# The end of a decoder step on one core: scaling of the output shared between VectorE and GpSimd, and a shorter path to the norm's factor

## The chip, the core and the metric

The kernel is written in Bass and runs on one core of one Trainium2 chip. The core has a matrix engine (TensorE, PE in the profile, PEld where it loads weights), a vector engine (VectorE, DVE), a scalar engine (ScalarE, ACT), a general engine (GpSimd, POOL) and a sequencer that only issues transfers (SyncE, SP). Engines wait for each other through semaphores. The metric is the device time of one execution in microseconds (us).

## The reference, cut to what matters

One layer of a hybrid decoder is computed for 256 prompt rows and 8 x 8 sample rows, together 320 tokens of width 2048: a norm, one wide input projection, three attention branches, three gated branch projections, an output projection with the residual added, and a final norm. The change is in the last step alone:

```
y = x + merged @ w_out                                     # (320, 2048)
inv = rsqrt(mean(y * y, axis=-1) + 1e-6)                    # one factor for each token
y_prompt, y_sample = y * inv * final_norm_g
```

## The kernel before, in words

Everything is transposed: the width lies on the 128 partitions in 16 blocks (KB), and the tokens lie along the free dimension. Weights come as a stream of tiles of 128 x 2048; ScalarE and VectorE split each tile into a high and a low part (lines 494 and 753), and TensorE multiplies high by high, high by low and low by high (lines 1263 to 1265). The output projection makes two of the 16 blocks per trip; VectorE adds each to the residual in y_t (line 1162), GpSimd squares it and adds the squares up in y_ss (lines 479 and 481), and ScalarE multiplies it by the gain of the final norm into y_out (line 718, semaphore y_gained).

The last two blocks are handled by hand, and in two halves of 160 tokens (h = 0 and h = 1), so that the final scaling of the first half can begin while TensorE still works on the second. In y_out a "half block" is thus 128 partitions x 160 tokens, there are 32 of them, and each is 81.92 KB in float32. For each half:

- VectorE adds the products to y_t (half_added, lines 1178 and 1179), adds the square of block 14 to the sums (rest_summed, line 1188) and squares block 15 (last_square, line 1193). ScalarE squares block 14 (line 728) and applies the gains (line 724).
- TensorE sums over the partitions by products with ones into two columns of the bank S0 (lines 1620, 1629, 1632; semaphore y_ssd): the tokens are then on the partitions, 128 in a column.
- VectorE makes mean + eps from them (mean, line 1199), ScalarE takes the square root (line 743), VectorE takes the reciprocal and makes one Newton step (newton, lines 1203 to 1206) and writes the result on the diagonal of a 128 x 128 matrix (y_diag, line 1210).
- TensorE multiplies ones by that diagonal (factor_products, line 1608; semaphore y_inv), which puts the factor of each token on all partitions of a bank: S1 for h = 0, P0 for h = 1.
- VectorE multiplies y_out by it in place, in ten parts (scaled, line 1217, the list OUT_PARTS of half, first and last block), reading the factor from PSUM, and SP stores each part when it is done (line 397).

The order on VectorE is written out by hand: newton(0), half_added(0, 1), scaled(0), rest_summed(1), half_added(1, 1), last_square(1), scaled(1), mean(1), scaled(2), newton(1), and then parts 3 to 9. Parts 0 to 4 are the first half of the tokens, 5 to 9 the second. GpSimd has nothing to do after its last sum of squares.

Of the kernel before, what the change touches and what calls it, by code (L numbers as in the profile page):

```python
# [12 lines left out]
P = 128  # L13
D_MODEL, SEQ, DEC_BATCH, DEC_SEQ, PAST, PAGE = 2048, 256, 8, 8, 256, 128
# [4 lines left out]
EPS = 1e-6  # L19
NEG = -1e30  # L20
KB = D_MODEL // P
# [13 lines left out]
NGP = 32  # L35
FIRST_SEQS = 5
HALF = TOK // 2
OUT_PARTS = ((0, 0, 2), (0, 2, 6), (0, 6, 8), (0, 8, 12), (0, 12, 16), (1, 0, 4), (1, 4, 8), (1, 8, 12), (1, 12, 14), (1, 14, 16))
HEAD = ((0, 2), (2, 4), (4, 8), (8, 12), (12, 16))

f32 = mybir.dt.float32
# [2 lines left out]
ALU = mybir.AluOpType  # L44
ACT = mybir.ActivationFunctionType
# [33 lines left out]
def build(nc, A):  # L79
    ctx = ExitStack()  # L80
    with ctx:
# [24 lines left out]
        ident = fixed("ident", [P, P])  # L106
        ones = fixed("ones", [P, P])
# [11 lines left out]
        st = fixed("st", [P, 16])  # L119
# [96 lines left out]
        y_last = fixed("y_last", [P, 4, HALF])  # L216
        y_sum = fixed("y_sum", [P, 2, HALF])
        y_diag = fixed("y_diag", [P, 2, P])

        bank = [ctx.enter_context(nc.psum_tensor(f"bank{n}", [P, 512], f32)) for n in range(8)]  # L220
        W, (S0, S1, S2, P0, P1, OB) = bank[:2], bank[2:]
# [5 lines left out]
        def two(name):  # L227
# [22 lines left out]
         brow_copied, bo_ready, bo_copied, pad_zero, new_zero, pc_zero, pb_zero, bias_in) = [  # L250
            sem(n) for n in ("b_staged kt_in vs_in bs_ready bvc_rdy bmax_rdy bexp_done bp_ready bpt_ready bpt_copied "
                             "brow_ready brow_copied bo_ready bo_copied pad_zero new_zero pc_zero pb_zero bias_in").split()]
        (oz_rdy, oz_hi_rdy, oz_lo_rdy, mrg_rdy, mrg_hi_rdy, mrg_lo_rdy, y_in, y_sums, y_half, y_put, y_pres, y_squared, y_ssd, y_v, y_r, y_turned, y_inv, y_gained, y_rdy, y_wr) = [
            sem(n) for n in ("oz_rdy oz_hi_rdy oz_lo_rdy mrg_rdy mrg_hi_rdy mrg_lo_rdy y_in y_sums y_half y_put y_pres y_squared y_ssd y_v y_r "
                             "y_turned y_inv y_gained y_rdy y_wr").split()]
        dve_chain = sem("dve_chain")
        carrier = sem("carrier")

# [32 lines left out]
        def _(sp):  # L291
# [100 lines left out]
                    load_keys(b + 2)  # L392
            weight_tile(1, J_MRG + 1)
            weight_tiles(J_MRG + 2, J_END)
            for n, (h, k0, k1) in enumerate(OUT_PARTS):
                sp.wait_ge(y_rdy, n + 1)
                sp.dma_start(A["y_out"][h, :, k0:k1, :], y_out[:, h, k0:k1, :]).then_inc(y_wr, 16)
            sp.wait_ge(y_wr, 16 * len(OUT_PARTS))


        @block.gpsimd
        def _(pool):
# [73 lines left out]
            with pool.Fori(0, KB // 2 - 1) as k:  # L476
                for u in range(2):
                    pool.wait_ge(w_free[u], k + (J_OUT + 2))
                    nc.gpsimd.tensor_tensor(y_sq[:, u, :], one(y_t, k * 2 + u), one(y_t, k * 2 + u), ALU.mult).then_inc(y_sums, 1)
                    pool.wait_ge(y_sums, k * 4 + (2 * u + 2))  # L480
                    nc.gpsimd.tensor_tensor(y_ss[:], y_ss[:], y_sq[:, u, :], ALU.add).then_inc(y_sums, 1)
            pool.wait_ge(win_wr, 16 * DEC_BATCH)
            pool.wait_ge(kv_out, 32)
            for u in range(2):
# [4 lines left out]
        def _(act):  # L489
# [226 lines left out]
            def gained_block(kb):  # L716
                act.wait_ge(w_free[kb % 2], kb // 2 + (J_OUT + 2))
                nc.scalar.activation(y_out[:, :, kb, :], y_t[:, kb, :].rearrange("p (h c) -> p h c", h=2), ACT.Copy,
                                     scale=gains[:, 2, kb:kb + 1]).then_inc(y_gained, 1)

            def gained_half(u, h):
                kb = KB - 2 + u
                act.wait_ge(y_put, 2 * h + u + 1)
                nc.scalar.activation(y_out[:, h, kb, :], y_t[:, kb, h * HALF:(h + 1) * HALF], ACT.Copy, scale=gains[:, 2, kb:kb + 1]).then_inc(y_gained, 1)

            def squared_half(h):
                act.wait_ge(y_put, 2 * h + 1)
                nc.scalar.activation(y_last[:, 2 * h, :], y_t[:, KB - 2, h * HALF:(h + 1) * HALF], ACT.Square).then_inc(y_squared, 1)
# [6 lines left out]
                        gained_block(2 * k - 2 + u)  # L735
            for kb in range(KB - 4, KB - 2):
                gained_block(kb)
            for h in range(2):
                squared_half(h)
                gained_half(0, h)  # L740
                gained_half(1, h)
                act.wait_ge(y_v, h + 1)
                nc.scalar.activation(st[:, 3:5], st[:, 0:2], ACT.Sqrt).then_inc(y_r, 1)


        @block.vector
        def _(dve):
# [447 lines left out]
            v, y, t = st[:, 0:2], st[:, 3:5], st[:, 6:8]  # L1195

            def mean(h):
                dve.wait_ge(y_ssd, h + 1)
                nc.vector.tensor_scalar(v, S0[:, 256 * h:256 * h + 2], 1.0 / D_MODEL, EPS, ALU.mult, ALU.add).then_inc(y_v, 1)

            def newton(h):
                dve.wait_ge(y_r, h + 1)
                ch.link(nc.vector.reciprocal(y, y))
                ch.link(nc.vector.scalar_tensor_tensor(t, y, -0.5, y, ALU.mult, ALU.mult))
                ch.link(nc.vector.tensor_tensor(t, t, v, ALU.mult))
                ch.link(nc.vector.scalar_tensor_tensor(y, t, 1.5, y, ALU.add, ALU.mult))
                if h:
                    dve.wait_ge(y_inv, 1)
                for n in range(2):
                    nc.vector.tensor_scalar_mul(y_diag[:, n, :], ident[:], st[:, 3 + n:4 + n]).then_inc(y_turned, 1)  # L1210

            def scaled(n):
                h, k0, k1 = OUT_PARTS[n]
                out = y_out[:, h, k0:k1, :]
                dve.wait_ge(y_gained, KB if h == 0 else KB + 2)
                dve.wait_ge(y_inv, h + 1)
                nc.vector.tensor_tensor(out, out, (S1, P0)[h][:, 0:HALF].unsqueeze(1).to_broadcast([P, k1 - k0, HALF]),
                                        ALU.mult).then_inc(y_rdy, 1)

            dve.wait_ge(y_half, 1)  # L1220
            ch.link(half_added(0, 0))
            dve.wait_ge(y_half, 2)
# [8 lines left out]
            mean(0)  # L1231
            newton(0)
            dve.wait_ge(y_half, 5)
            half_added(0, 1).then_inc(y_put, 1)
# [3 lines left out]
            half_added(1, 1).then_inc(y_put, 1)  # L1238
            last_square(1).then_inc(y_pres, 1)
            scaled(1)  # L1240
            mean(1)
            scaled(2)
            newton(1)
            scaled(3)
            scaled(4)
            for n in range(5, len(OUT_PARTS)):
                scaled(n)


# [1 line left out]
        def _(pe):  # L1251
# [350 lines left out]

            firsts = (0, HALF - P)

            def factor_products(h):
                for n, (c0, c1) in enumerate(((0, P), (P, HALF))):
                    pe.wait_ge(y_turned, 2 * h + n + 1)
                    mm = nc.tensor.matmul((S1, P0)[h][:, c0:c1], ones[:], y_diag[:, n, P - (c1 - c0):P], start=True, stop=True)
                mm.then_inc(y_inv, 1)

            for u in range(2):
# [12 lines left out]
            factor_products(0)  # L1624
            half_part(1, 1, range(9, KB))
            pe.wait_ge(y_v, 1)
            pe.wait_ge(y_pres, 2)
# [3 lines left out]
            for n, first in enumerate(firsts):  # L1631
                mm = nc.tensor.matmul(S0[:, 256 + n:257 + n], y_last[:, 3, first:first + P], ones[:, 0:1], start=False, stop=True, skip_group_check=True)
            mm.then_inc(y_ssd, 1)
            factor_products(1)


# [107 lines left out]
```

## Time and profile before

| what | value |
|---|---|
| median of 3 runs | 1124.12 us (1123.13 to 1125.02) |
| the profiled execution's own time | 1123.93 us |
| its span, first to last instruction | 1122.1 us |
| time outside the span | 1.83 us |
| PE busy | 1110.0 us (99%) |
| DVE busy | 620.2 us (55%) |
| ACT busy | 422.4 us (38%) |
| POOL busy | 63.6 us (6%) |
| granted TensorE clock, mean | 0.996 |

The time is that of a whole execution; the rows of the trace count from the start of the span. Busy time says how long an engine had work, not whether that work set the end. In the rows, names are those of the program (bank stands for any PSUM bank), and "[0.69 <-DVE y_last L1193]" is the idle time before an instruction and what ended it. A float32 product of TensorE shows as two records.

### The profile page before, as it was taken

How to read it: one execution, taken by the hardware profiler on the slowest of the kernel's cores; microseconds unless marked ns; L12 is line 12 of the kernel's file. 1: busy time of each engine (PE TensorE's matmuls, PEld its weight loads, DVE VectorE, ACT ScalarE, POOL GpSimd, SP SyncE). 2: the span in 40 equal slices, each digit the busy share in tenths (PEclk: the TensorE clock that was granted, in tenths of full speed). 3: DMA queues.
4: the chain of work that ended last, by engine and by line, in shares of the span. 5: the costliest groups of instructions: out<-in, count | busy, mean ns of one | idle time of the engine just before them, and what ended most of it. 6: DMA issues, size and time to landing. Idle time of an engine off the chain costs nothing.

```text
span 1122.1 us, 19565 instructions
## 1 busy us (share of the span) xinstructions
PE 1110.0 (99%) x8092; PEld 1086.1 (97%) x8092; DVE 620.2 (55%) x914; ACT 422.4 (38%) x573; POOL 63.6 (6%) x111
## 2 busy tenths in 40 slices
PE   9999999999999999999999999999999999999996
PEld 7998999999999999999999999999999999999996
DVE  5974443536446767675555567454454454454445
ACT  6633322424335445443333334333333333333332
POOL 0014000000000000000000000000000000002220
PEclk9999999999999999999999999999999999999998
DMA  8545775544545233349787834544444444464442
GB/s 289 191 168 193 245 262 192 188 149 151 172 137 185 79 114 109 114 162 311 246 299 262 271 121 167 171 168 168 170 168 169 169 150 149 151 243 148 150 150 94
DMA packets 63467, 201.79 MB, mean 180 GB/s; under 512 B 6448, under 2 KB 35184, under 8 KB 45088
## 3 DMA queue, kind: packets, MB, share of 16 engines
q1 hardware_dynamic: 58688, 186.50, 48.4%
q0 software_dynamic: 2400, 10.89, 2.8%
q10 hardware_dynamic: 2304, 3.34, 0.9%
q8 instruction: 55, 0.90, 0.3%
q14 instruction: 20, 0.16, 0.0%
HBM read 193.48 MB, written 11.41 MB: 183 GB/s over the span
## 4 chain that ended last, share of the span: by engine, by line
PE 92%; DVE 4%; DMA 2%; ACT 1%; issue 1%; SPq 1%; DVEq 0%; ACTq 0%
PE bank L1263 26%; PE bank L1265 26%; PE bank L1264 26%; DMA raw<-in_stream 2%; DVE w_lo L753 1%; PE bank L1594 1%; PE bank L1368 1%; PE bank L1363 1%; PE bank L1340 1%; PE bank L1342 1%; PE bank L1341 1%; PE bank L1490 1%; DVE m_lo L780 1%; ACT w_hi L494 1%; PE bank L1425 0%
## 5 line engine op out<-in xcount | busy, mean ns | idle before, releaser
L494 ACT ACTIVATE w_hi<-raw 128x2048 fp32r<-128x2048 f32 x141 | 270.0, 1915 | 580.5 <-PE bank L1265 535.6
L1263 PE MATMUL bank<-h_hi,w_hi 128*128 128x320 f32 x1552 | 484.9, 312 | 0.5 <-DVE w_lo L753 0.5
L1265 PE MATMUL bank<-h_hi,w_lo 128*128 128x320 f32 x1552 | 479.6, 309 | 0.0
L1264 PE MATMUL bank<-h_lo,w_hi 128*128 128x320 f32 x1552 | 479.5, 309 | 0.0
L753 DVE TENSOR_TENSOR w_lo<-raw,w_hi 128x2048 fp32r<-128x2048 f32 x141 | 327.6, 2323 | 178.5 <-ACT w_hi L494 178.4
L1263 PEld LDWEIGHTS bank<-h_hi,w_hi 128*128 128x128 f32 x1552 | 291.5, 188 | 5.4 <-issue 3.9
L1264 PEld LDWEIGHTS bank<-h_lo,w_hi 128*128 128x128 f32 x1552 | 291.5, 188 | 0.4
L1265 PEld LDWEIGHTS bank<-h_hi,w_lo 128*128 128x128 f32 x1552 | 291.3, 188 | 0.0
L1264 PE MATMUL bank<-oz_lo,w_hi 128*128 128x320 f32 x256 | 78.9, 308 | 0.0
L1265 PE MATMUL bank<-oz_hi,w_lo 128*128 128x320 f32 x256 | 78.8, 308 | 0.0
L1263 PE MATMUL bank<-oz_hi,w_hi 128*128 128x320 f32 x256 | 78.8, 308 | 0.0
L1263 PE MATMUL bank<-mrg_both,w_hi 128*128 128x320 f32 x224 | 69.0, 308 | 0.0
L1264 PE MATMUL bank<-mrg_both,w_hi 128*128 128x320 f32 x224 | 69.0, 308 | 0.0
L1265 PE MATMUL bank<-mrg_both,w_lo 128*128 128x320 f32 x224 | 69.0, 308 | 0.0
L1137 DVE TENSOR_TENSOR g<-bank,inv 128x320 f32<-128x320 f32 x32 | 15.7, 490 | 72.2 <-PE bank L1265 72.2
L1263 PEld LDWEIGHTS bank<-oz_hi,w_hi 128*128 128x128 f32 x256 | 48.0, 188 | 0.0
L1264 PEld LDWEIGHTS bank<-oz_lo,w_hi 128*128 128x128 f32 x256 | 48.0, 188 | 0.0
L1265 PEld LDWEIGHTS bank<-oz_hi,w_lo 128*128 128x128 f32 x256 | 48.0, 188 | 0.0
L1263 PEld LDWEIGHTS bank<-mrg_both,w_hi 128*128 128x128 f32 x224 | 42.0, 188 | 0.0
L1264 PEld LDWEIGHTS bank<-mrg_both,w_hi 128*128 128x128 f32 x224 | 42.0, 188 | 0.0
L1265 PEld LDWEIGHTS bank<-mrg_both,w_lo 128*128 128x128 f32 x224 | 42.0, 188 | 0.0
L1094 DVE TENSOR_TENSOR g_t<-bank,inv 128x320 f32<-128x320 f32 x16 | 7.9, 492 | 42.4 <-PE bank L1265 42.4
(341 smaller groups left out, 1137.7 us busy)
## 6 DMA issues: line engine op xcount, KB each, us to landing
raw<-in_stream SPq DMA_DIRECT2D x141, 1024.0 KB, 5.0
cmp_t<-in_cmp_pages SPq DMA_DIRECT2D x32, 128.0 KB, 4.2
kt_moba<-in_moba_k SPq DMA_DIRECT2D x16, 256.0 KB, 5.3
kt_mem<-in_mem_k SPq DMA_DIRECT2D x8, 512.0 KB, 6.2
vs_moba<-in_moba_v SPq DMA_DIRECT2D x16, 256.0 KB
vs_mem<-in_mem_v SPq DMA_DIRECT2D x8, 512.0 KB
out_win_old<-in_cache_win POOLq DMA_DIRECT2D x8, 512.0 KB, 3.6
raw<-in_stream SPq DMA_DIRECT2D x11, 256.0 KB, 9.1
```

Source lines behind the costliest of these rows:

```text
L494: nc.scalar.activation(w_hi[:, u], raw[:, u], ACT.Copy).then_inc(hi_ready[u], 1)
L753: nc.vector.tensor_tensor(w_lo[:, u], raw[:, u], w_hi[:, u].bitcast(f32), ALU.subtract).then_inc(lo_ready[u], 1)
L780: nc.vector.scalar_tensor_tensor(lo[:, kb, :], x[:, kb, :], gains[:, gain, kb:kb + 1], hi[:, kb, :].bitcast(f32), ALU.mult, ALU.subtract). ...
L1137: nc.vector.tensor_tensor(g12[:, u, br, :], W[u][:, 0:TOK], inv[:], ALU.mult).then_inc(w_free[u], 1)
L1263: nc.tensor.matmul(out[:, 0:n], w_hi[:, u, kb, :], hi[:, kb, :], start=(kb == first), stop=False)
L1264: nc.tensor.matmul(out[:, 0:n], w_hi[:, u, kb, :], lo[:, kb, :], start=False, stop=False)
L1265: mm = nc.tensor.matmul(out[:, 0:n], w_lo[:, u, kb, :], hi[:, kb, :], start=False, stop=(kb == last))
L1340: nc.tensor.matmul(out[:], m_hi[:, kb, rows], high, start=(kb == 0), stop=False)
L1341: nc.tensor.matmul(out[:], m_lo[:, kb, rows], high, start=False, stop=False)
L1342: mm = nc.tensor.matmul(out[:], m_hi[:, kb, rows], low, start=False, stop=(kb == KB - 1))
L1363: nc.tensor.matmul(out[:, 0:used], w_hi[:, 1, s, :], c_hi[:, s, 0:used], start=(s == 0), stop=False, skip_group_check=True)
L1368: mm = nc.tensor.matmul(out[:, 0:used], w_lo[:, 1, s, :], c_hi[:, s, 0:used], start=False, stop=(s == CMP_STRIDE - 1), skip_group_check=True)
```

## The change

OUT_PARTS is split in two lists. VectorE keeps 18 half blocks in six parts, GpSimd gets 14 in three. The factor of each half is also copied by ScalarE from PSUM to a tile y_fac in SBUF, which GpSimd reads, and VectorE too for the first half; for the second half VectorE reads P0 as before, and TensorE makes the factor a second time in P1 for the copy. The square root is taken on ScalarE straight from the sums in PSUM, with 1 / D_MODEL as its scale and eps as its bias. The last operation of the Newton step is done by the instruction that writes the diagonal. TensorE makes five products of ones between the last sums and the factor. SP stores eight of the nine parts in the order DVE 0, DVE 1, POOL 0, POOL 1, DVE 2 to 5; ScalarE's queue stores POOL 2.

```diff
-OUT_PARTS = ((0, 0, 2), (0, 2, 6), (0, 6, 8), (0, 8, 12), (0, 12, 16), (1, 0, 4), (1, 4, 8), (1, 8, 12), (1, 12, 14), (1, 14, 16))
+OUT_DVE = ((0, 0, 2), (0, 2, 6), (1, 4, 8), (1, 8, 12), (1, 12, 14), (1, 14, 16))
+OUT_POOL = ((0, 6, 11), (0, 11, 16), (1, 0, 4))
...
+        y_fac = fixed("y_fac", [P, 2, HALF])
...
@@ sync
-            for n, (h, k0, k1) in enumerate(OUT_PARTS):
-                sp.wait_ge(y_rdy, n + 1)
+            def store(ready, parts, n):
+                h, k0, k1 = parts[n]
+                sp.wait_ge(ready, n + 1)
                 sp.dma_start(A["y_out"][h, :, k0:k1, :], y_out[:, h, k0:k1, :]).then_inc(y_wr, 16)
+            for n in range(2):
+                store(y_rdy, OUT_DVE, n)
+            for n in range(2):
+                store(y_rdy_pool, OUT_POOL, n)
+            for n in range(2, len(OUT_DVE)):
+                store(y_rdy, OUT_DVE, n)
...
@@ gpsimd, after the last sum of squares
+            def scaled(n):
+                h, k0, k1 = OUT_POOL[n]
+                out = y_out[:, h, k0:k1, :]
+                pool.wait_ge(y_gained, KB if h == 0 else KB + 2)
+                pool.wait_ge(y_fac_rdy, h + 1)
+                nc.gpsimd.tensor_tensor(out, out, y_fac[:, h, :].unsqueeze(1).to_broadcast([P, k1 - k0, HALF]), ALU.mult).then_inc(y_rdy_pool, 1)
+
+            for n in range(len(OUT_POOL)):
+                scaled(n)
...
@@ scalar
+            def factor_out(h):
+                act.wait_ge(y_inv, 2 * h + 1)
+                nc.scalar.activation(y_fac[:, h, :], (S1, P1)[h][:, 0:HALF], ACT.Copy).then_inc(y_fac_rdy, 1)
+
             for h in range(2):
                 squared_half(h)
+                if h:
+                    factor_out(0)
                 gained_half(0, h)
                 gained_half(1, h)
-                act.wait_ge(y_v, h + 1)
-                nc.scalar.activation(st[:, 3:5], st[:, 0:2], ACT.Sqrt).then_inc(y_r, 1)
+                act.wait_ge(y_ssd, h + 1)
+                nc.scalar.activation(st[:, 3:5], S0[:, 256 * h:256 * h + 2], ACT.Sqrt, scale=1.0 / D_MODEL, bias=st[:, 13:14]).then_inc(y_r, 1)
+            factor_out(1)
+            act.wait_ge(y_rdy_pool, 3)
+            h, k0, k1 = OUT_POOL[2]
+            act.dma_start(A["y_out"][h, :, k0:k1, :], y_out[:, h, k0:k1, :]).then_inc(y_wr, 16)
...
@@ vector
             def mean(h):
-                dve.wait_ge(y_ssd, h + 1)
                 nc.vector.tensor_scalar(v, S0[:, 256 * h:256 * h + 2], 1.0 / D_MODEL, EPS, ALU.mult, ALU.add).then_inc(y_v, 1)
...
                 ch.link(nc.vector.reciprocal(y, y))
+                mean(h)
                 ch.link(nc.vector.scalar_tensor_tensor(t, y, -0.5, y, ALU.mult, ALU.mult))
-                ch.link(nc.vector.tensor_tensor(t, t, v, ALU.mult))
-                ch.link(nc.vector.scalar_tensor_tensor(y, t, 1.5, y, ALU.add, ALU.mult))
+                nc.vector.tensor_scalar(t[:, 0:1], t[:, 0:1], v[:, 0:1], 1.5, ALU.mult, ALU.add)
+                ch.link(nc.vector.tensor_scalar(t[:, 1:2], t[:, 1:2], v[:, 1:2], 1.5, ALU.mult, ALU.add))
...
-                    nc.vector.tensor_scalar_mul(y_diag[:, n, :], ident[:], st[:, 3 + n:4 + n]).then_inc(y_turned, 1)
+                    nc.vector.tensor_scalar(y_diag[:, n, :], ident[:], y[:, n:n + 1], t[:, n:n + 1], ALU.mult, ALU.mult).then_inc(y_turned, 1)
...
-                h, k0, k1 = OUT_PARTS[n]
+                h, k0, k1 = OUT_DVE[n]
...
-                dve.wait_ge(y_inv, h + 1)
-                nc.vector.tensor_tensor(out, out, (S1, P0)[h][:, 0:HALF].unsqueeze(1).to_broadcast([P, k1 - k0, HALF]),
+                dve.wait_ge((y_fac_rdy, y_inv)[h], h + 1)
+                nc.vector.tensor_tensor(out, out, (y_fac[:, 0, :], P0[:, 0:HALF])[h].unsqueeze(1).to_broadcast([P, k1 - k0, HALF]),
                                         ALU.mult).then_inc(y_rdy, 1)
...
             last_square(1).then_inc(y_pres, 1)
             scaled(1)
-            mean(1)
-            scaled(2)
             newton(1)
-            scaled(3)
-            scaled(4)
-            for n in range(5, len(OUT_PARTS)):
+            for n in range(2, len(OUT_DVE)):
                 scaled(n)
...
@@ tensor, after the last sums
-            factor_products(1)
+            for n in range(5):
+                nc.tensor.matmul(W[0][:, 0:P], ones[:], ones[:], start=True, stop=True)
+            factor_products(1, P0)
+            factor_products(1, P1)
```

## Rows read from the trace of the kernel before

**Rows 1.** Chain of waits, its last piece: start us, us, what.

```profile
1117.48 1.53 DVE y_out L1217 x3
```

**Rows 2.** Table of stretches: busy us of each engine, PEclk, DMA share, GB/s.

```profile
1112.00:1113.50 1.50, 0.61 (x4) 0.52 (x4) 1.47 (x6) 0.42 (x2) 0.00 (x0) 1.00 0.00 0
1113.50:1115.10 1.60, 0.68 (x4) 0.69 (x4) 1.50 (x6) 0.00 (x0) 0.00 (x0) 0.50 0.80 307
1115.10:1116.10 1.00, 0.38 (x3) 0.24 (x2) 1.00 (x3) 0.00 (x0) 0.00 (x0) 0.50 0.00 0
1116.10:1121.30 5.20, 0.00 (x0) 0.00 (x0) 2.90 (x5) 0.00 (x0) 0.00 (x0) 0.50 0.97 377
```

**Rows 3.** Stores of the output: an issue on the timeline, all ten, time to landing.

```profile
1115.31 0.33 SPq L397 DMA_DIRECT2D out_y_out<-y_out  x1
...
L397 SPq DMA_DIRECT2D out_y_out<-y_out x10: 332/332/739, 1110.5 to 1119.1; - x10
...
DMA to landing us min/median/max: 1.8/2.3/2.7
```

**Rows 4.** Timeline of DVE from 1110 us: start us, us, line, operation.

```profile
1110.03 0.49 DVE L1217 TENSOR_TENSOR y_out<-y_out,bank 128x320 f32<-128x320 f32 x1 [0.45 <-PE bank L1608]
1110.43 0.32 DVE L1188 TENSOR_TENSOR y_sum<-y_ss,y_last 128x160 f32<-128x160 f32 x1
1111.07 0.33 DVE L1178 SCALAR_TENSOR_TENSOR y_t<-bank,y_t 128x160 f32<-128x160 f32 x1 [0.32 <-PE bank L1594]
...
1111.79 0.32 DVE L1193 TENSOR_TENSOR y_last<-y_t 128x160 f32<-128x160 f32 x1
1112.03 0.81 DVE L1217 TENSOR_TENSOR y_out<-y_out,bank 128x640 f32<-128x640 f32 x1
1112.81 0.16 DVE L1199 TENSOR_SCALAR st<-bank 128x2 f32<-128x2 f32 x1
...
1113.29 0.16 DVE L1203 RECIPROCAL st<-st 128x2 f32<-128x2 f32 x1
...
1114.08 0.48 DVE L1210 TENSOR_SCALAR y_diag<-ident,st 128x128 f32<-128x128 f32 x2
1114.47 4.53 DVE L1217 TENSOR_TENSOR y_out<-y_out,bank 128x640 f32<-128x640 f32 x7
```

**Rows 5.** Timeline of PE at the end, and of its first products of ones.

```profile
1109.39 0.53 PE L1608 MATMUL bank<-y_diag,ones 128*128 128x128 f32 x4
...
1112.16 0.61 PE L1632 MATMUL bank<-ones,y_last 128*128 128x1 f32 x4 [0.69 <-DVE y_last L1193]
1114.42 1.06 PE L1608 MATMUL bank<-y_diag,ones 128*128 128x128 f32 x4 [1.65 <-DVE y_diag L1210]
...
1.72 6.62 PE L1281 MATMUL bank<-ones 128*128 128x128 f32 x32 [1.72 <-DVE ones L761]
```

**Rows 6.** Timeline of ACT: a square of 160 tokens and the square root.

```profile
1109.61 0.34 ACT L728 ACTIVATE y_last<-y_t 128x160 f32<-128x160 f32 x1 [1.93 <-DVE y_t L1179]
...
1113.00 0.21 ACT L743 ACTIVATE st<-st 128x2 f32<-128x2 f32 x1 [0.79 <-DVE st L1199]
```

**Rows 7.** Groups of POOL instructions, shapes apart: busy us, mean ns of one.

```profile
L481 POOL TENSOR_TENSOR y_ss<-y_ss,y_sq 128x320 f32<-128x320 f32 x14 | 12.3, 880 | 1.1
...
L460 POOL COPY kt_moba<-k_smp 128x32 f32<-128x32 f32 x8 | 1.7, 208 | 0.0
```

**Rows 8.** Timelines of POOL and DVE: a w_lo that starts beside POOL, and one alone.

```profile
1083.44 0.88 POOL L481 TENSOR_TENSOR y_ss<-y_ss,y_sq 128x320 f32<-128x320 f32 x1
...
1083.84 2.63 DVE L753 TENSOR_TENSOR w_lo<-raw,w_hi 128x2048 fp32r<-128x2048 f32 x1 [1.40 <-ACT w_hi L494]
...
900.82 2.29 DVE L753 TENSOR_TENSOR w_lo<-raw,w_hi 128x2048 fp32r<-128x2048 f32 x1 [1.51 <-ACT w_hi L494]
```

**Rows 9.** Timelines of DVE and POOL: a POOL copy that starts beside w_lo.

```profile
518.22 2.28 DVE L753 TENSOR_TENSOR w_lo<-raw,w_hi 128x2048 fp32r<-128x2048 f32 x1
...
519.58 0.99 POOL L459 COPY kt_nsa<-k_smp 128x32 f32<-128x32 f32 x1 [18.31 <-PE bank L1483]
```

More of the change, by code:

```diff
@@ L252, in build @@
                              "brow_ready brow_copied bo_ready bo_copied pad_zero new_zero pc_zero pb_zero bias_in").split()]
-        (oz_rdy, oz_hi_rdy, oz_lo_rdy, mrg_rdy, mrg_hi_rdy, mrg_lo_rdy, y_in, y_sums, y_half, y_put, y_pres, y_squared, y_ssd, y_v, y_r, y_turned, y_inv, y_gained, y_rdy, y_wr) = [
+        (oz_rdy, oz_hi_rdy, oz_lo_rdy, mrg_rdy, mrg_hi_rdy, mrg_lo_rdy, y_in, y_sums, y_half, y_put, y_pres, y_squared, y_ssd, y_v, y_r, y_turned, y_inv, y_fac_rdy, y_gained, y_rdy, y_rdy_pool, y_wr) = [
             sem(n) for n in ("oz_rdy oz_hi_rdy oz_lo_rdy mrg_rdy mrg_hi_rdy mrg_lo_rdy y_in y_sums y_half y_put y_pres y_squared y_ssd y_v y_r "
-                             "y_turned y_inv y_gained y_rdy y_wr").split()]
+                             "y_turned y_inv y_fac_rdy y_gained y_rdy y_rdy_pool y_wr").split()]
         dve_chain = sem("dve_chain")
@@ L394, in _ @@
             weight_tiles(J_MRG + 2, J_END)
-            for n, (h, k0, k1) in enumerate(OUT_PARTS):
-                sp.wait_ge(y_rdy, n + 1)
+            def store(ready, parts, n):
+                h, k0, k1 = parts[n]
+                sp.wait_ge(ready, n + 1)
                 sp.dma_start(A["y_out"][h, :, k0:k1, :], y_out[:, h, k0:k1, :]).then_inc(y_wr, 16)
-            sp.wait_ge(y_wr, 16 * len(OUT_PARTS))
+            for n in range(2):
[4 more added lines that the diff above has]
+                store(y_rdy, OUT_DVE, n)
+            sp.wait_ge(y_wr, 16 * (len(OUT_DVE) + len(OUT_POOL)))
         @block.gpsimd
@@ L1209, in newton @@
                 for n in range(2):
-                    nc.vector.tensor_scalar_mul(y_diag[:, n, :], ident[:], st[:, 3 + n:4 + n]).then_inc(y_turned, 1)
+                    nc.vector.tensor_scalar(y_diag[:, n, :], ident[:], y[:, n:n + 1], t[:, n:n + 1], ALU.mult, ALU.mult).then_inc(y_turned, 1)
             def scaled(n):
-                h, k0, k1 = OUT_PARTS[n]
+                h, k0, k1 = OUT_DVE[n]
                 out = y_out[:, h, k0:k1, :]
                 dve.wait_ge(y_gained, KB if h == 0 else KB + 2)
-                dve.wait_ge(y_inv, h + 1)
-                nc.vector.tensor_tensor(out, out, (S1, P0)[h][:, 0:HALF].unsqueeze(1).to_broadcast([P, k1 - k0, HALF]),
+                dve.wait_ge((y_fac_rdy, y_inv)[h], h + 1)
+                nc.vector.tensor_tensor(out, out, (y_fac[:, 0, :], P0[:, 0:HALF])[h].unsqueeze(1).to_broadcast([P, k1 - k0, HALF]),
                                         ALU.mult).then_inc(y_rdy, 1)
+            nc.vector.memset(st[:, 13:14], EPS)
             dve.wait_ge(y_half, 1)
@@ L1230, in _ @@
             nc.vector.tensor_tensor(y_sum[:, 0, :], y_sum[:, 0, :], y_last[:, 1, :], ALU.add).then_inc(y_pres, 1)
-            mean(0)
             newton(0)
@@ L1603, in _, with factor_products @@
             firsts = (0, HALF - P)
-            def factor_products(h):
+            def factor_products(h, out):
                 for n, (c0, c1) in enumerate(((0, P), (P, HALF))):
                     pe.wait_ge(y_turned, 2 * h + n + 1)
-                    mm = nc.tensor.matmul((S1, P0)[h][:, c0:c1], ones[:], y_diag[:, n, P - (c1 - c0):P], start=True, stop=True)
+                    mm = nc.tensor.matmul(out[:, c0:c1], ones[:], y_diag[:, n, P - (c1 - c0):P], start=True, stop=True)
                 mm.then_inc(y_inv, 1)
@@ L1623, in _ @@
             half_part(1, 1, range(0, 9))
-            factor_products(0)
+            factor_products(0, S1)
             half_part(1, 1, range(9, KB))
```

## The prediction

> **What bounds the kernel now.** TensorE is busy for 99% of the span, but the change touches only what comes after its last large product, so I read the end alone. The chain of waits ends in VectorE's scaling [rows 1]. That names an engine, not yet the limit, so the table of stretches comes next [rows 2]: from 1116.1 to 1121.3 us the DMA engines are 97% busy at 377 GB/s. Ten stores are issued, the last at 1119.1, and each lands 1.8 to 2.7 us after its issue [rows 3]. VectorE scales the last 24 half blocks in 4.53 us [rows 4], 0.19 us each; the transfer takes 5.2 us for the same 24 (24 x 81.92 KB = 1.97 MB), 0.217 us each. So from 1116.1 on the store is the slower of the two, and the span ends 0.8 us after it has drained. The issue that restarts it is at 1115.31, the data follow 0.8 us later.
>
> The reader is to see that the DMA engines stand still from 1112.0 to 1113.5 and from 1115.1 to 1116.1 [rows 2]. A change gains only by filling these holes with ready half blocks. For any new order
>
> end of span = issue that restarts the stream + 0.8 + 0.217 x half blocks left + holes + 0.8.
>
> Check on before: 1115.3 + 0.8 + 5.2 + 0.8 = 1122.1.
>
> **The edits, one by one.**
>
> *Root straight from the sums.* The mean starts at 1112.81 [rows 4], the root at 1113.00 [rows 6]: 0.19 us leave the path. The mean then runs behind the reciprocal, inside the 0.2 us that a linked step takes.
>
> *End of the refinement in the diagonal.* From reciprocal to diagonal 0.79 us now, four linked steps of 0.2 [rows 4]. Then three linked steps and two short unlinked instructions, which I price by their spacing at 0.07 each: 0.74. Bounds: 0.6 (the two free) and 0.9 (a full 0.16 each). Gain 0.05.
>
> *PE kept warm.* The same factor products take 0.53 us in the first half and 1.06 in the second [rows 5]; the granted clock is 1.00 until 1113.5 and 0.50 behind it [rows 2], that is 2.4 and then 1.2 GHz, after TensorE had little to do since 1111 and nothing between 1112.77 and 1114.42. If the clock holds, 0.5 us is gained. The five products are ten records; 32 such records took 6.62 us at the start [rows 5], so ten take up to 2.1 us. They are hidden only while the diagonal comes later than that behind the sums.
>
> *The second factor product and the copy.* Behind the first, 0.5 to 1.1 us on TensorE (warm, cold); only GpSimd's third part waits for it. The copy is 160 wide: 0.34 us by the square of that width [rows 6]; from below 0.21, the root of two elements. For the first half it is on the path: scaled(0) now starts at 1110.03 [rows 4], right behind the product, and would start at 1110.4. The stores must start there, and rest_summed(1) is queued behind it on VectorE.
>
> *GpSimd's parts.* Its add of 320 elements takes 0.88 us, a copy of 32 elements 0.21 [rows 7]: 2.1 ns an element. A part of 800: 0.88 + 480 x 2.1 ns = 1.9 us; from above 2.2, all of it in proportion. The part of 640: 1.55 us. Two parts need 3.8 us. They can begin at 1110.5 and no engine waits for GpSimd there; the cover looks ample. VectorE keeps 12 half blocks behind the second factor, 2.3 us instead of 4.5.
>
> **The port.** Here the profile speaks against the change. A w_lo subtraction with both inputs in SBUF takes 2.29 us alone. The one that starts at 1083.84, while GpSimd adds until 1084.32, takes 2.63 [rows 8]: 0.34 us more for 0.48 us of overlap, and the other twelve w_lo from 1013 us on are stretched in the same way. The reverse shows as well: a GpSimd copy that takes 0.21 us [rows 7] takes 0.99 when it starts inside w_lo, and ends at 520.57, 0.07 us behind it [rows 9]. Neither engine shares; the later one waits for the rest of the other's instruction.
>
> The Trainium skill, "SBUF — State Buffer", section "Who interferes with whom", states this as a rule: a VectorE instruction with two SBUF inputs and a GpSimd instruction that reads SBUF contend, and "Whoever issues first gets the shared pair for the whole instruction"; the trace agrees in both directions. A plain bandwidth view would give rival 2 below instead.
>
> Which VectorE instructions between 1110.4 and 1115 have two SBUF inputs? scaled(0) and scaled(1), which lose their PSUM operand by the change; rest_summed(1), last_square(1), and the first step of newton(1) (y by y). All stand ahead of the second factor. The scaling of the second half reads PSUM and is free.
>
> **The sum.** Factor ready 1110.35; scaled(0) to 1110.9; rest_summed(1) directly behind it to 1111.1. GpSimd takes the port and has it to 1112.9. half_added(1, 1) needs no port and is done at 1111.8, but last_square(1) waits and ends at 1113.1 instead of 1112.1. GpSimd's second part has asked since 1112.9 and runs from 1113.0 to 1114.85; scaled(1) waits for it and ends at 1115.5 (1112.84 now). The sums are there at 1113.75 (0.61 us of TensorE, [rows 5]), the root at 1114.0, so neither is late; newton(1) starts behind scaled(1), the diagonal at 1116.3. From diagonal to factor it is 1.40 us now (1114.08 to 1115.48). TensorE would stand idle from 1111.5 to 1113.15 ahead of the last sums, against 0.69 us now [rows 5], so I take the cold price; the products of ones (1113.8 to 1115.9) are hidden before the diagonal: factor at 1117.7, the first second-half part at 1118.5.
>
> SP stores in a fixed order, so the two finished GpSimd parts stand behind scaled(1). The restart is at 1115.6 with 30 half blocks left; 14 are ready and last to 1119.4, when the next are there. End: 1115.6 + 0.8 + 6.5 + 0.8 = 1123.7. GpSimd's third part: factor again 1118.3 to 1118.8, copy 0.35, a start 0.1 later (as VectorE's behind TensorE, 1109.92 to 1110.03 [rows 4, 5]), 1.55, so 1120.3 to 1120.8, landed by 1123.2: inside. That is +1.6 us. If instead scaled(1) gets the port before GpSimd's second part, it ends at 1113.9, but newton's first step waits until 1115.5 and the first second-half part comes at 1118.3; 16 half blocks remain from 1119.2: 1123.5, or +1.4. Both orders cost about 1.5 us. The profiled execution (1123.93) stands 0.19 below the median; on the median this gives 1124.12 + 1.5 = **1125.6 us**. A measurement of this kernel tells 0.2%, 2.25 us, from no change, so the forecast is "no change that can be told", on the slow side.
>
> **Rivals.**
>
> *1. GpSimd wins the port right behind scaled(0)* (slower). It decides at 1110.8, where rest_summed(1) and GpSimd both ask. If GpSimd is first, rest_summed(1) ends at 1112.9, half_added(1, 1) at 1113.5, last_square(1) waits for the second part until 1114.8, the sums come at 1115.5. TensorE is then cold and the ten records hold it until 1117.6, past the diagonal (1116.5); the factor comes at 1118.5, the first second-half part at 1119.4, and 16 half blocks end at 1120.2 + 3.5 + 0.8 = 1124.5: +2.4, 1126.5 us. If GpSimd keeps the port through both parts it is +3.3, 1127.4. For it: GpSimd asks from 1110.5 on. Against it: VectorE's instructions follow each other without a gap (1110.03 and 1110.43 overlap, [rows 4]). No row shows both asking at once. Chance 0.25.
>
> *2. The port matters little* (GpSimd's reads leave gaps, or it starts late). Then scaled(1) ends at 1113.2, restart at 1113.3 with 30 left: 1113.3 + 0.8 + 6.5 + 0.8 = 1121.4. The factor is 0.25 + 0.5 us earlier and never late. -0.7 us, 1123.4. Note how small the gain is: the DMA stream takes back what three engines save. The port's rows speak against it [rows 8, 9]. Chance 0.2.
>
> *3. The clock does not hold, or holds better.* Inside the forecast a warm factor brings 0.5 us only if the stream has a hole there; it has none in my first order. So 0 to -0.5: 1125.1 to 1125.6. It changes no sign.
>
> **From the cases to the numbers.** Forecast 0.5, rival 1 0.25, rival 2 0.2, and 0.05 for something unseen in either direction. Below 1121.9 (faster) lies almost nothing, since even rival 2 stops at 1123.4: 0.03. Above 1126.4 lies most of rival 1 and the upper bound of GpSimd's price (0.3 us more for each of two parts): 0.25. The rest, 0.72, is within. The range takes in rival 2 less a little noise of the median, and rival 1 with its dearer end: 1123.0 to 1127.3.
>
> **What would show it.** Right: last_square(1) and scaled(1), or newton's first step, stretched to 1 to 2.5 us and ending with GpSimd's parts; GpSimd's 800-wide parts near 1.9 us; the DMA engines idle until about 1116 and then at 97% to the end; the diagonal near 1116.3. Wrong: last_square(1) at 0.32 us beside a running GpSimd; or rest_summed(1) stretched (rival 1); or a restart of the stores before 1113.5 (rival 2); a factor product of 0.53 us in the second half would show the warm clock.

## The result, and the profile after

The changed kernel takes 1126.96 us (median of 10 runs, 1125.81 to 1129.33), the kernel before 1123.76 us on the same chip (10 runs, 1123.06 to 1125.67). The ratio is 1.0031, with a 95% interval of 1.0023 to 1.0039: **slower by 3.2 us**, clear of noise, and more than the 0.2% bound of the prediction. The profiled execution took 1126.42 us with a span of 1124.6 us; the one before took 1123.93 with 1122.1.

Because the end of the last large product shifts from execution to execution, all runs below are also compared by their **tail**: from the end of that product to the end of the span. Timeline of PE of the kernel before, the last group of large products:

```profile
1109.76 1.27 PE L1594 MATMUL bank<-mrg_both,w_hi 128*128 128x320 f32 x7
```

It ends at 1111.03, so the tail of before is 1122.1 - 1111.03 = 11.1 us. A tail is read from the one profile of each kernel, a median from all its executions. Now the timeline of PE of the changed kernel:

```profile
1109.03 1.27 PE L1620 MATMUL bank<-mrg_both,w_hi 128*128 128x320 f32 x7
1112.18 0.58 PE L1655 MATMUL bank<-ones,y_sum 128*128 128x1 f32 x4 [1.88 <-DVE y_sum L1218]
1114.01 0.65 PE L1658 MATMUL bank<-ones,y_last 128*128 128x1 f32 x4 [1.24 <-DVE y_last L1223]
1114.51 2.48 PE L1661 MATMUL bank<-ones 128*128 128x128 f32 x10
1116.79 1.49 PE L1634 MATMUL bank<-y_diag,ones 128*128 128x128 f32 x8
```

The large products end at 1110.30, the tail is 14.3 us: 3.2 us longer, as much as the medians differ. TensorE waits 1.88 us for VectorE ahead of the first sums and 1.24 ahead of the last, where it waited only ahead of the last, 0.69 [rows 5]. What VectorE did meanwhile (timeline of DVE, changed kernel):

```profile
1109.63 0.49 DVE L1247 TENSOR_TENSOR y_out<-y_out,y_fac 128x320 f32<-128x320 f32 x1 [0.75 <-ACT y_fac L760]
1110.05 1.99 DVE L1218 TENSOR_TENSOR y_sum<-y_ss,y_last 128x160 f32<-128x160 f32 x1
...
1112.66 1.29 DVE L1223 TENSOR_TENSOR y_last<-y_t 128x160 f32<-128x160 f32 x1
1113.88 0.81 DVE L1247 TENSOR_TENSOR y_out<-y_out,y_fac 128x640 f32<-128x640 f32 x1
1114.98 0.17 DVE L1232 RECIPROCAL st<-st 128x2 f32<-128x2 f32 x1 [0.30 <-ACT st L769]
...
1115.82 0.60 DVE L1240 TENSOR_SCALAR y_diag<-ident,st 128x128 f32<-128x128 f32 x2
1117.80 2.35 DVE L1247 TENSOR_TENSOR y_out<-y_out,bank 128x640 f32<-128x640 f32 x4 [1.38 <-PE bank L1634]
```

The same add takes 1.99 us instead of 0.32 and the same square 1.29 instead of 0.32 [rows 4]. Their ends, 1112.04 and 1113.95, lie 0.2 us behind those of GpSimd's two parts (timeline of POOL, changed kernel: the first two as one group, then the second alone, then the third):

```profile
1109.67 4.09 POOL L498 TENSOR_TENSOR y_out<-y_out,y_fac 128x800 f32<-128x800 f32 x2 [12.01 <-ACT y_fac L760]
...
1111.82 1.95 POOL L498 TENSOR_TENSOR y_out<-y_out,y_fac 128x800 f32<-128x800 f32 x1
...
1118.76 1.54 POOL L498 TENSOR_TENSOR y_out<-y_out,y_fac 128x640 f32<-128x640 f32 x1 [4.99 <-ACT y_fac L760]
```

The view of the program's last line shows the closing drain of GpSimd's queue (duration in ns, min/median/max, then its start):

```profile
L82 POOLq DRAIN  x1: 5337/5337/5337, 1119.1 to 1119.1; - x1
```

The chain of waits no longer ends in VectorE's scaling [rows 1] but in GpSimd's third part (its last piece in the changed kernel), and the table of stretches shows the stores standing still around it:

```profile
1118.76 1.54 POOL y_out L498
```

```profile
1113.00:1114.60 1.60, 0.59 (x5) 0.60 (x5) 1.60 (x2) 0.09 (x1) 0.77 (x1) 0.95 0.00 0
1114.60:1117.00 2.40, 2.40 (x12) 2.40 (x12) 1.42 (x8) 0.26 (x1) 0.00 (x0) 0.50 0.61 238
1118.70:1119.40 0.70, 0.00 (x0) 0.00 (x0) 0.70 (x2) 0.00 (x0) 0.64 (x1) 1.00 0.00 0
1119.40:1123.10 3.70, 0.00 (x0) 0.00 (x0) 0.74 (x2) 0.00 (x0) 0.90 (x1) 0.75 0.95 354
```

After the first small store nothing moves until the stream restarts within the second row, there is a hole from 1118.7 to 1119.4, and the last byte is out by 1123.1. The span ends 1.5 us later, where it ended 0.8 us later before [rows 2]. So there were two things to explain: the held rows, and a late end that the stores do not account for.

SP's fixed order adds to the first hole: GpSimd's first part is done at about 1111.9 and waits behind VectorE's second, done at 1114.69. No run changes that order alone. The hole at 1118.7 argues that it did not set the end, because the stream had already run out of finished parts there.

### The profile page after: what moved, and what is told of

Read it like the earlier page. It is cut to its first block, busy times and chain, and to the rows that moved or that the text cites. A ratio compares the mean times of both kernels' runs of the same rounds, so it can differ in the third digit from the quotient of the medians.

```text
span 1124.6 us, 19593 instructions
## 1 busy us (share of the span) xinstructions
PE 1111.4 (99%) x8106; PEld 1087.6 (97%) x8106; DVE 620.6 (55%) x911; ACT 422.9 (38%) x575; POOL 69.2 (6%) x114
## 4 chain that ended last, share of the span: by engine, by line
PE 97%; DVE 1%; DMA 1%; ACT 0%; issue 0%; SPq 0%; POOL 0%; POOLq 0%; DVEq 0%; ACTq 0%
PE bank L1289 27%; PE bank L1290 27%; PE bank L1291 27%; PE bank L1394 1%; PE bank L1389 1%; DMA x_t<-in_x_t 1%; PE bank L1366 1%; PE bank L1367 1%; PE bank L1368 1%; PE bank L1312 1%; PE bank L1516 1%; PE bank L1620 1%; PE bank L1451 0%; PE bank L1509 0%; PE bank L1391 0%; PE bank L1626 0%
```

## Experiments

Theory P: the port. GpSimd's reads of SBUF hold VectorE's instructions with two SBUF inputs. Rivals: the products of ones, the copy and the second factor product, or GpSimd's work as such.

**Reads beside VectorE, nothing else changed**, and **fills at the same place**. The kernel before, with this on GpSimd behind its last sum (scr and scf are scratch, cleared by GpSimd ahead of this, not shown):

```diff
...
+            pool.wait_ge(y_inv, 1)
+            for n in range(2):
+                nc.gpsimd.tensor_tensor(scr[:], scr[:], scf[:].unsqueeze(1).to_broadcast([P, 5, HALF]), ALU.mult).then_inc(scr_rdy, 1)
+                pool.wait_ge(scr_rdy, n + 3)
```

and in the second run, in place of the products:

```diff
...
+            for n in range(4):
+                nc.gpsimd.memset(scr[:], 0.0).then_inc(scr_rdy, 1)
+                pool.wait_ge(scr_rdy, n + 3)
```

> The kernel before with nothing taken from it; GpSimd alone gets two products of 800 elements on scratch tiles, from the first factor on, at the place of its first two parts in the changed kernel. Theory (the SBUF port): GpSimd starts at about 1110.1 us, ahead of the add of the squares (0.32 us now), which is held until about 1112; the square of block 15 is held by the second product until about 1113.9 instead of ending at 1112.1; diagonal, factor and the last 24 half blocks move with it: +1.9 us on the whole (1.5 to 2.3), with no other part of the change in it. Rival (the loss comes from the products of ones and from the copy of the factor): 0, and both VectorE rows stay at 0.32 us.

> The same place, but four fills of 800 elements on scratch: GpSimd is busy for about 3 us and reads nothing. Theory (the port is that of reads): 0, both VectorE rows at 0.32 us. Rival (any work of GpSimd beside VectorE costs, or writes collide too): +1 to +2 us, rows stretched as in the run with reads.

Measured: reads 1125.49 us against 1123.22, ratio 1.0021 (1.0012 to 1.0030), that is +2.3 us; tail 13.1, +2.0. Fills 1123.04, ratio 1.0000 (0.9991 to 1.0009), tail 11.1. Timelines of DVE and POOL, the run with reads:

```profile
1109.96 1.71 DVE L1198 TENSOR_TENSOR y_sum<-y_ss,y_last 128x160 f32<-128x160 f32 x1
...
1112.30 1.33 DVE L1203 TENSOR_TENSOR y_last<-y_t 128x160 f32<-128x160 f32 x1
...
1109.60 3.85 POOL L490 TENSOR_TENSOR scr<-scr,scf 128x800 f32<-128x800 f32 x2 [10.79 <-PE bank L1618]
```

The same with fills:

```profile
1108.98 0.32 DVE L1198 TENSOR_TENSOR y_sum<-y_ss,y_last 128x160 f32<-128x160 f32 x1
...
1110.32 0.32 DVE L1203 TENSOR_TENSOR y_last<-y_t 128x160 f32<-128x160 f32 x1
...
1108.59 3.23 POOL L490 MEMSET scr<- 128x800 f32 x4 [10.76 <-PE bank L1618]
```

Two products that nobody reads cost about two thirds of the loss; 3.2 us of fills cost nothing that can be told. Theory P stands, and it is the reads that count.

**GpSimd later.** The changed kernel, with one wait more ahead of each part:

```diff
                 pool.wait_ge(y_fac_rdy, h + 1)
+                pool.wait_ge(y_pres, 3)
```

> The changed kernel, but GpSimd starts only when the square of block 15 is done. Theory: the add and the square are back at 0.33 us and the last sums come 1.9 us earlier; part (0, 2, 6) of VectorE gets the port first, GpSimd's first part follows and now holds the first step of the Newton step until it ends, so that about 1.5 us of the 3.2 come back: 1.3 to 2 us faster than the changed kernel, about 1 us slower than the one before. Rival (what counts is that GpSimd's parts are done early): slower than the changed kernel, since its first two parts end 2 us later.

Measured: 1126.39 us, ratio to before 1.0027 (1.0016 to 1.0037); tail 13.8, half a microsecond better than the changed kernel, not 1.3 to 2. The add and the square are back at 0.32 and 0.33 us and the Newton step is held, as expected. What I had not foreseen is in the last row (timeline of DVE):

```profile
1111.20 0.82 DVE L1248 TENSOR_TENSOR y_out<-y_out,y_fac 128x640 f32<-128x640 f32 x1
...
1112.56 1.21 DVE L1235 SCALAR_TENSOR_TENSOR st<-st 128x2 f32<-128x2 f32 x1
1113.81 0.21 DVE L1236 TENSOR_SCALAR st<-st 128x1 f32<-128x1 f32 x1
...
1114.18 1.48 DVE L1241 TENSOR_SCALAR y_diag<-ident,st 128x128 f32<-128x128 f32 x1
```

The first write of the diagonal, with one SBUF tensor and two scalars from SBUF, takes 1.48 us and ends with GpSimd's second part; the steps of one element between them are not held. So the add and the square are freed of 1.7 + 1.0 us of waiting, and the Newton step and the diagonal take on 1.1 + 1.2 us, all on the same path (one write of the diagonal takes 0.35 us alone).

**Without the products of ones.**

```diff
-            for n in range(5):
-                nc.tensor.matmul(W[0][:, 0:P], ones[:], ones[:], start=True, stop=True)
```

> The changed kernel without the five products of ones. They run from 1114.5 to 1116.9 us there, at 1.2 GHz from the start, and the diagonal is written by 1116.15 and 1116.4. Theory: the factor products start at 1116.2 instead of 1116.8 or later, and take 0.9 to 1.1 us cold: 0.6 us faster than the changed kernel, that is +2.6 us against before. Rival (the products of ones warm the clock for what follows and pay for themselves): the same time or slower.

Measured: 1127.05 us, ratio to before 1.0032 (1.0020 to 1.0045), the same as the changed kernel; tail 14.6. A miss of the expectation, and the run does not decide it: in its profile the clock fell earlier, the last sums took 1.01 us instead of 0.65, and the root came 0.4 us later, while from the diagonal to the first factor it took 1.6 us instead of 2.0. The gain that the rows show (0.4 us) and the loss of that execution cancel.

**The ones alone, in the kernel before** (the same loop ahead of factor_products(1)).

> The kernel before with the five products of ones and nothing else. They would run from 1112.8 us to 1114.2 or 1114.9 there, the diagonal comes at 1114.4. If they keep the clock at 2.4 GHz, the factor products take 0.53 to 0.63 us instead of 1.06, if not, they start up to 0.5 us later. Theory (the stream of stores is the limit and has 640 KB of the first half in front of it): the time is the same within the interval either way. Rival (the factor is on the path): 0.5 us faster or slower.

Measured: 1123.47 us, ratio 1.0002 (0.9993 to 1.0011), tail 11.15. Ones and factor products (timeline of PE), and the same factor products in the run b5_tail_op below, which has no ones:

```profile
1112.15 1.36 PE L1635 MATMUL bank<-ones 128*128 128x128 f32 x10
1113.94 0.63 PE L1608 MATMUL bank<-y_diag,ones 128*128 128x128 f32 x4 [0.43 <-DVE y_diag L1210]
```

```profile
1114.55 0.63 PE L1614 MATMUL bank<-y_diag,ones 128*128 128x128 f32 x4 [1.65 <-DVE y_diag L1216]
```

The factor products are fast with them, 0.63 us. But they are as fast in b5 without them, after the same 1.65 us of idle that left them at 1.06 us in the profile of before [rows 5]; of the two runs on scratch, also without ones and with 1.65 us of idle, the one with fills has 0.63 and the one with reads 1.06. The table of stretches of b5 shows why: the granted clock is 1.00 (2.4 GHz) in this stretch, and in before it had fallen to 0.50 at 1113.5 [rows 2].

```profile
1114.50:1115.20 0.70, 0.63 (x4) 0.52 (x4) 0.70 (x2) 0.00 (x0) 0.00 (x0) 1.00 0.87 326
```

So one profile cannot say whether the ones kept the clock. What is shown: warm or cold, the tail of the kernel before stays at 11.1 us; and in the profile of the changed kernel they ran at the lower clock (0.50 in the row from 1114.6). In the run with GpSimd later they ran fast (1.36 us), and the factor products, after 2.55 us of idle, were slow all the same (eight records in 1.92 us).

**The root alone, in the kernel before** (ScalarE's activation straight from S0, the mean behind the reciprocal, as in the change).

> The kernel before with the root taken straight from the sums, the mean behind the reciprocal, and nothing else. Theory: 0.2 us leave the path of the root, but the reciprocal waits for part (0, 6, 8) on VectorE until 1113.3 anyway and the mean adds 0.08, so 0 to -0.1 us. Rival (the step counts in full): -0.25 us. Both lie within what a measurement tells; the rows decide, by the time from the last sums to the diagonal, 1.3 us now.

Measured: 1123.03 us, ratio 0.9999 (0.9990 to 1.0008), tail 11.1. Timeline of DVE:

```profile
1112.04 0.16 DVE L1202 RECIPROCAL st<-st 128x2 f32<-128x2 f32 x1
...
1112.89 0.48 DVE L1210 TENSOR_SCALAR y_diag<-ident,st 128x128 f32<-128x128 f32 x2
```

From the last sums to the diagonal it takes 1.23 us (1111.66 to 1112.89) instead of 1.31, inside the 0 to 0.1 us expected, and nothing is gained at the end. The mean behind the reciprocal is not free: reciprocal to diagonal takes 0.85 us here and 0.79 in the kernel before.

**The last store from SP.** The changed kernel, with GpSimd's third part stored by SP as its last; the store on ScalarE's queue is gone.

```diff
             for n in range(2, len(OUT_DVE)):
                 store(y_rdy, OUT_DVE, n)
+            store(y_rdy_pool, OUT_POOL, 2)
...
-            act.wait_ge(y_rdy_pool, 3)
-            h, k0, k1 = OUT_POOL[2]
-            act.dma_start(A["y_out"][h, :, k0:k1, :], y_out[:, h, k0:k1, :]).then_inc(y_wr, 16)
```

> The changed kernel, but SP's queue stores GpSimd's third part too, as its last one. In the changed kernel the stream drains at about 1123.1 us and the span ends 1.5 us later, where it was 0.8 us before; the store on ScalarE's queue lands 3.2 us after its issue, those of SP in 1.8 to 2.7. Theory (the other queue's landing sets the end): 0.5 to 0.8 us faster than the changed kernel, 2.5 us slower than before. Rival (the end is late because that part is late, whoever stores it): the same time.

Measured: 1127.34 us, ratio to before 1.0036 (1.0022 to 1.0050), tail 15.0: nothing gained, the theory falls. In this profile the last sums again took 1.01 us instead of 0.65. SyncE's waits, GpSimd's third part and the drain of its queue in that run:

```profile
SPq L82 <- DMA out_y_out<-y_out: 2.3, 1, 2.3
SPq L82 <- PEq L82: 1.2, 1, 1.2
```

```profile
1119.43 1.54 POOL L499 TENSOR_TENSOR y_out<-y_out,y_fac 128x640 f32<-128x640 f32 x1 [5.62 <-ACT y_fac L761]
```

```profile
L82 POOLq DRAIN  x1: 5336/5336/5336, 1119.7 to 1119.7; - x1
```

When the last store has landed, SP waits another 1.2 us at the common end of all engines (0.2 us in the run with reads, for one), and that end follows the drain of GpSimd: it runs from 1119.7 to 1125.04, span 1125.3. GpSimd's third part ended at 1120.97. In the changed kernel: part to 1120.30, drain to 1124.4, span 1124.6. In all four profiles with a third part (the changed kernel, GpSimd later, no ones, and this one) the span ends 4.3 us behind that part. In the run with reads the drain begins on an idle GpSimd and takes 4.07 us:

```profile
L81 POOLq DRAIN  x1: 4066/4066/4066, 1113.6 to 1113.6; - x1
```

New theory D: the drain needs 4.07 us from the end of GpSimd's last instruction, whatever the stores do.

**One small product at the very end of the kernel before.**

```diff
+            nc.gpsimd.memset(scr[:], 0.0).then_inc(scr_rdy, 1)
+            pool.wait_ge(scr_rdy, 1)
+            pool.wait_ge(y_rdy, len(OUT_PARTS))
+            nc.gpsimd.tensor_tensor(scr[:], scr[:], scr[:], ALU.mult).then_inc(scr_rdy, 1)
```

> The kernel before with one more instruction: GpSimd multiplies 32 elements of scratch when VectorE's last part is done (1119.0 us on the clock of before), 0.2 us of work that nothing waits for. In every run so far GpSimd's closing drain ends 4.07 us after its last instruction, and the third part of the changed kernel ends 4.1 us ahead of it and 4.3 us ahead of the end of the span. Theory (the drain ends the changed kernel, not its stores): the instruction ends at about 1119.4, the drain at 1123.5, the span at 1123.7: +1.6 us. Rival (GpSimd's drain lies beside the stores and the end waits for those): 0.

Measured: 1125.08 us against 1123.57, ratio 1.0013 (1.0004 to 1.0022), +1.5 us; tail 12.7, +1.6. Timeline of POOL and its drain:

```profile
1119.28 0.24 POOL L487 TENSOR_TENSOR scr<-scr 128x32 f32<-128x32 f32 x1 [20.68 <-DVE y_out L1223]
```

```profile
L81 POOLq DRAIN  x1: 4066/4066/4066, 1119.6 to 1119.6; - x1
```

0.24 us of work on nothing, and the tail is 1.6 us longer. Theory D stands.

**The changed kernel without GpSimd's third part.**

```diff
-OUT_DVE = ((0, 0, 2), (0, 2, 6), (1, 4, 8), (1, 8, 12), (1, 12, 14), (1, 14, 16))
-OUT_POOL = ((0, 6, 11), (0, 11, 16), (1, 0, 4))
+OUT_DVE = ((0, 0, 2), (0, 2, 6), (1, 0, 4), (1, 4, 8), (1, 8, 12), (1, 12, 14), (1, 14, 16))
+OUT_POOL = ((0, 6, 11), (0, 11, 16))
...
-            factor_out(1)
...
-            factor_products(1, P1)
```

> The changed kernel without GpSimd's third part: VectorE scales (1, 0, 4) from P0 first of its second half, SP stores it, and the second factor product, its copy and ScalarE's store are gone. GpSimd keeps both parts of the first half, and with them every hold of the port. Theory (drain): the span ends with the stream again, 0.8 us behind its last byte instead of 1.5 to 2.0; VectorE's 16 half blocks take 3.1 us from the same factor, faster than the stream; 0.7 to 0.9 us faster than the changed kernel, and about 2.3 us slower than before, which is what the port alone cost in the run with reads on scratch. Rival (GpSimd's third part helps): slower than the changed kernel.

Measured: 1126.21 us, ratio to before 1.0024 (1.0014 to 1.0034), +2.6 us; tail 13.85, 0.45 less than the changed kernel, against 0.7 to 0.9 expected. Its last sums ran at half clock (1.01 us instead of 0.65), which takes back some 0.36 of it. SP's last wait is 0.2 us again, so its end is that of the stream. The direction is as the theory has it, but the intervals of the two ratios overlap, so the size of the gain is not shown by the times.

**The port kept free: three versions.** From the kernel before; the main edits of c1:

```diff
+OUT_PARTS = ((0, 0, 2), (0, 2, 6), (0, 6, 8), (0, 13, 16), (1, 0, 2), (1, 2, 6), (1, 6, 10), (1, 10, 14), (1, 14, 16))
+OUT_POOL = (0, 8, 13)
...
-            rest_summed(1).then_inc(y_pres, 1)
...
-            last_square(1).then_inc(y_pres, 1)
...
+                    act.wait_ge(y_put, 4)
+                    nc.scalar.activation(y_last[:, 3, :], y_t[:, KB - 1, HALF:TOK], ACT.Square).then_inc(y_squared, 1)
...
-                nc.tensor.matmul(S0[:, 256 + n:257 + n], y_sum[:, 1, first:first + P], ones[:, 0:1], start=(n == 0), stop=False, skip_group_check=True)
+                nc.tensor.matmul(S0[:, 256 + n:257 + n], y_ss[:, HALF + first:HALF + first + P], ones[:, 0:1], start=(n == 0), stop=False, skip_group_check=True)
...
+                nc.tensor.matmul(S0[:, 256 + n:257 + n], y_last[:, 2, first:first + P], ones[:, 0:1], start=False, stop=False, skip_group_check=True)
```

VectorE scales the first half from PSUM as before, but behind ScalarE's copy, so that only one engine reads that bank at a time.

> Made from the kernel before, with the port kept free for VectorE's path. TensorE adds y_ss and both squares itself, ScalarE squares block 15, so VectorE has no instruction with two SBUF inputs until the Newton step; GpSimd scales five half blocks of the first half (8 to 13) from a copy of the factor and is done before that step; the root is taken straight from the sums; no products of ones, no second factor product. Theory (GpSimd helps where it holds nothing that VectorE wants, and the stream of stores is the limit): the part of five takes 1.9 us and ends at about 1112.3 on the clock of before, the stream restarts at 1113 instead of 1116, has a hole of about 1 us ahead of the second half, and the span ends 0.7 to 1.2 us earlier than before. Rival (GpSimd costs wherever it reads): as slow as before or slower.

> As the run c1, with GpSimd's work in two parts of three half blocks (8 to 11, 11 to 14), so that the first is ready to store 0.7 us earlier, and one half block less for VectorE ahead of the second factor. Theory (the stream is the limit, its holes are what can be gained): the first hole shrinks by 0.5 to 0.7 us, a later one may grow; from the end of the last large product to the end of the span 9.5 to 9.8 us, where c1 has 9.96 and before 11.07; 1.0 to 1.5 us faster than before. Rival (the second factor decides, and the time of the first half counts for nothing): as c1.

> As c2 with the five products of ones between the last sums and the factor. At 2.4 GHz they take 1.36 us (as in the run with ones alone) and end just before the diagonal; where the clock falls they take 2.4 us and make the factor later by up to 0.4. Theory: the same time as c2 within 0.3 us, since either outcome moves the factor by less than the stream has in front of it. Rival (they are worth their place once the factor is on the path): 0.4 us faster than c2.

| run | median, before | ratio (interval) | tail |
|---|---|---|---|
| c1_free_port | 1122.67, 1123.33 | 0.9993 (0.9984 to 1.0002) | 9.96 |
| c2_free_port | 1122.59, 1123.57 | 0.9992 (0.9983 to 1.0001) | 9.9 |
| c3_free_port_ones | 1122.51, 1123.57 | 0.9991 (0.9982 to 1.0000) | 9.9 |

One of the 11 executions of c1 took 3889.06 us, which no trace explains; without it the median is 1122.44.

Timelines of POOL and DVE of c2, and its drain:

```profile
1109.46 2.38 POOL L493 TENSOR_TENSOR y_out<-y_out,y_fac 128x480 f32<-128x480 f32 x2 [11.99 <-ACT y_fac L754]
...
1110.72 1.21 DVE L1235 TENSOR_TENSOR y_out<-y_out,bank 128x640 f32<-128x640 f32 x2
1112.17 0.17 DVE L1220 RECIPROCAL st<-st 128x2 f32<-128x2 f32 x1 [0.24 <-ACT st L761]
...
1112.45 0.15 DVE L1222 SCALAR_TENSOR_TENSOR st<-st 128x2 f32<-128x2 f32 x1
```

```profile
L82 POOLq DRAIN  x1: 6141/6141/6141, 1109.8 to 1109.8; - x1
```

GpSimd scales six half blocks in 2.38 us while VectorE scales six others in 1.21 at full speed. GpSimd is done at 1111.8, ahead of VectorE's first step with two SBUF inputs (1112.45), and its drain is over by 1116. All three profiles have a tail 1.1 to 1.2 us shorter than before, and all three medians are lower, by 0.7, 1.0 and 1.1 us; each interval alone touches no change. Taken together, without the long execution, their median is 0.95 us below that of the 58 executions of the kernel before, 0.6 to 1.3 by resampling; the three were put together after the results were known. Against the changed kernel, measured in another set of runs, they are some 4 us faster. The first hole got smaller from c1 to c2, but the tail did not. That speaks for the rival of c2, that the second factor decides there: in all three profiles the span ends 6.0 to 6.1 us behind the last factor product. The ones make no difference (9.9 and 9.9), and the factor products take 0.63 us with and without them.

What these three do not show is GpSimd's share of the gain. They also move the sums to TensorE and a square to ScalarE, and no run makes these edits with VectorE scaling all 32 half blocks.

## Why the prediction was right in its mechanism and wrong in its likeliest case

The measured time lies inside the range (1127.0 in 1123.0 to 1127.3), but the forecast of +1.5 us was half of what came, and "no change that can be told" had 0.72 of the chance where slower came true. Point by point:

- *The port*, read from rows 8 and 9, was right: the add and the square are held to the end of GpSimd's parts, fills do not hold them, reads alone cost 2.3 us. The Trainium skill ("SBUF — State Buffer", section "Who interferes with whom") has it that a VectorE instruction with two SBUF inputs collides with GpSimd's reads and not with its mere writes; both runs on scratch agree (1.71 and 1.33 us beside reads, 0.32 and 0.32 beside fills).
- *The step that failed* is the order at the port: "rest_summed(1) directly behind it to 1111.1. GpSimd takes the port and has it to 1112.9." GpSimd had asked since 1109.67 and got the port as scaled(0) ended; rest_summed(1), which follows it on VectorE without a gap, waited and took 1.99 us. That is rival 1, to which I gave 0.25. I held VectorE's instructions that overlap by 0.08 us to keep the port between them; no row had shown that. The reverse holds too: the waiting add got in between GpSimd's two parts, though these also follow each other without a gap (it ends at 1112.04, the second part runs from 1111.82 to 1113.77).
- *Rival 1's course*, on a clock 0.73 us earlier: add held to 1112.2 (measured 1112.04), square to 1114.1 (1113.95), cold ones until 1116.9 (1116.99), factor 1117.8 (VectorE starts on it at 1117.80), end 1123.8. Measured 1124.6. The 0.8 us left are a term that the sum put at nothing: the drain of 4.07 us behind GpSimd's last instruction. The prediction had the third part "inside" because its store landed in time.
- *Luck*: the range reached up to 1127.3 for a course that did not happen, GpSimd keeping the port through both parts. Rival 1 as it came stands at 1126.5 in the prediction; the measured 1126.96 is inside only because that room was there for the drain, which nobody had priced.
- *The durations* held: 1.95 us for 800 elements (1.9; 2.2 for the first part, with its wait for scaled(0)), 1.54 for 640 (1.55), 0.30 for the copy (0.34).
- *The refinement in the diagonal* was priced at -0.05 us and costs a little. Reciprocal to diagonal is 0.84 us in the changed kernel and 0.85 in the run with the root alone, which has the old refinement, so it gains 0.01 there; the steps with a scalar from SBUF take 0.21 each (0.16 assumed at most). The two writes of the diagonal take 0.60 instead of 0.48 [rows 4]. Small, but of the wrong sign. The mean behind the reciprocal, which the prediction had put inside a linked step for nothing, adds 0.06 (0.85 against 0.79).
- *The ones*: cold in the changed kernel, as taken; 2.35 us on the path, of which about 0.4 could be saved by the rows of the run without them; its time shows no gain.
- *The stream as the limit* was right where it was used: root and ones alone change nothing, and filling its holes with the port free (c2) gives 1.1 us of tail, less than the 1.8 us of VectorE's work that was taken off (six half blocks at 0.19 us, two instructions of 0.32).
- *What is left*: of the 3.2 us of tail, the run with reads has 2.0 and the drain, by the sum above, 0.8. The last 0.4 us no run separates; the copy of the factor is among them, for which VectorE's first part waits 0.75 us instead of 0.45 [rows 4].

## What to carry to other kernels

Before GpSimd is given work, list VectorE's instructions beside it that read two SBUF tensors (and writes of a diagonal from one, as here), and assume that each will wait for GpSimd's instruction to end, the first one too: in these profiles an engine that asked while the other worked was next. Move the inputs to PSUM, or the work to ScalarE and TensorE, or end GpSimd's part before that stretch. Let nothing of GpSimd's be among the last instructions of a kernel: its closing drain took 4.07 us here behind even 0.24 us of work, and it ends the kernel once it outlasts the stores.

## What the runs showed of the hardware that was not expected

- GpSimd's closing drain: 4066 ns each time that it began on an idle engine (the two runs with scratch work and the small product at the end); in the changed kernel, where it began during the third part, it ended 4.1 us behind it.
- A write of 128 x 128 from one SBUF tensor with scalars from SBUF is held by GpSimd's reads as well (1.48 us in the run with GpSimd later, 0.35 alone); steps of one element with such scalars are not (0.21 us).
- The port goes to the engine that has asked, between two instructions of the other that follow each other without a gap: so in all four profiles of the changed kernel's order (the changed kernel, no ones, the store from SP, two parts: 1.99 us for the add each time).
- After the same 1.65 us of idle in the same code, TensorE's granted clock was 0.50 in one execution (the kernel before) and 1.00 in another (the run with the small product at the end).
